# A hybrid attention and RWKV-7 step on one core: projection in other groups of tiles, two products at other places of the recurrence's tile

## What is computed

```python
proj = rms_norm(h, norm_gain) @ w_in            # 2048 prompt rows and 8 x 16 sample rows
att, rcols, g_r = split_projection(proj)        # rcols: 1664 columns
xs = rcols + (prev - rcols) * mix               # prev: the row before, or the stored one
r, k, v, wd, ad = split(xs)
kk = heads(k * k_k)
kk = kk * rsqrt(maximum(sum(kk * kk), 1e-24))   # the sum of squares
y, S = wkv_scan(r, decay, k, v, kk, a, state0)  # the recurrence, per head 64 x 64
y = group_norm(y)
y = y + sum(r * k * r_k) * v                    # the bonus
```

## Time and profile before

| | us |
|---|---|
| median of 3 runs | 1923.75 |
| their range | 1923.07 to 1924.39 |
| the profiled execution | 1919.17 |
| its span, first to last instruction | 1917.4 |
| TensorE busy in the span | 1751.9 (91%) |
| VectorE busy | 859.5 (45%) |
| ScalarE busy | 775.8 (40%) |
| GpSimd busy | 351.7 (18%) |

### The profile page before, as it was taken

The page is one execution under the profiler, slowest core; times in us unless marked ns, Lnnn a source line. Parts: engine busy times, 40 slices in busy tenths (PEclk is TensorE's granted clock), DMA queues, the critical chain, the costliest instruction groups (busy, mean ns, idle before and its releaser), DMA issues. The chain is left out here.

```text
span 1917.4 us, 48732 instructions
## 1 busy us (share of the span) xinstructions
PE 1751.9 (91%) x21474; PEld 1408.2 (73%) x21474; DVE 859.5 (45%) x1195; ACT 775.8 (40%) x1635; POOL 351.7 (18%) x252
## 2 busy tenths in 40 slices
PE   5899999999996999999479999999999998279999
PEld 4677788877885888889357777777777777157787
DVE  5245545455543411211255566556655564143432
ACT  4455555556554321212344444444434431034421
POOL 3010100001000000000123453345334442200000
PEclk9999999999998999999679999999999999679999
DMA  6011111002115412111331212121212110266642
GB/s 220 28 51 34 50 34 50 29 34 67 34 34 203 138 68 93 61 50 43 113 124 48 83 48 60 48 82 48 59 49 82 48 42 22 94 257 237 225 162 105
DMA packets 110977, 160.84 MB, mean 84 GB/s; under 512 B 36272, under 2 KB 70192, under 8 KB 110512
## 3 DMA queue, kind: packets, MB, share of 16 engines
q1 hardware_dynamic: 101408, 143.25, 23.0%
q10 hardware_dynamic: 9360, 14.49, 2.1%
HBM read 103.18 MB, written 55.05 MB: 83 GB/s over the span
## 5 line engine op out<-in xcount | busy, mean ns | idle before, releaser
L935 PE MATMUL j_ps<-j_x_hi,j_w_hi 128*128 128x512 f32 (+1 forms) x520 | 191.3, 368 | 14.6 <-DVE j_x_lo L900 14.6
L935 PE MATMUL j_ps<-j_x_hi,j_w_lo 128*128 128x512 f32 (+1 forms) x520 | 191.0, 367 | 0.0
L935 PE MATMUL j_ps<-j_x_lo,j_w_hi 128*128 128x512 f32 (+1 forms) x520 | 191.0, 367 | 0.0
L565 PE MATMUL a_ps_proj<-a_w_hi,a_x_hi 128*128 128x512 f32 x384 | 158.6, 413 | 2.9 <-ACT a_qk L314 2.8
L565 PE MATMUL a_ps_proj<-a_w_hi,a_x_lo 128*128 128x512 f32 x384 | 158.8, 414 | 0.0
L565 PE MATMUL a_ps_proj<-a_w_lo,a_x_hi 128*128 128x512 f32 x384 | 156.2, 407 | 0.0
L918 DVE SCALAR_TENSOR_TENSOR j_out<-j_ps,j_rest,j_part 128x512 f32<-128x512 f32 (+1 forms) x65 | 43.6, 671 | 238.0 <-ACT j_last_cols L874 208.5
L244 POOL TENSOR_TENSOR a_x_lo<-a_xT,a_x_hi 128x1024 fp32r<-128x1024 f32 x17 | 41.5, 2443 | 486.2 <-ACT a_x_hi L300 486.2
L935 PEld LDWEIGHTS j_ps<-j_x_hi,j_w_hi 128*128 128x128 f32 x520 | 98.5, 189 | 31.0 <-issue 14.8
L2114 PE MATMUL o_ps_y<-o_w_hi,o_z_hi 128*128 128x512 f32 x272 | 111.2, 409 | 7.6 <-DVE o_y L2037 4.0
L1816 PE MATMUL r_ps_gate<-r_gate_w_hi,r_gate_x_hi 128*128 128x512 f32 x272 | 115.3, 424 | 2.3 <-POOL r_gate_x_lo L1339 1.5
(11 more groups left out here) (274 smaller groups left out, 4046.8 us busy)
## 6 DMA issues: line engine op xcount, KB each, us to landing
r_xs<-scratch_xs_T SPq DMA_DIRECT2D x17, 832.0 KB, 6.1
scratch_xs_T<-j_out ACTq DMA_DIRECT2D x52, 256.0 KB, 2.0
scratch_xT<-a_xT SPq DMA_DIRECT2D x17, 512.0 KB, 4.8
r_gate_x_raw<-scratch_xT SPq DMA_DIRECT2D x17, 512.0 KB, 6.7
scratch_gates<-r_gate_out SPq DMA_DIRECT2D x34, 256.0 KB, 2.4
o_g<-scratch_gates SPq DMA_DIRECT2D x17, 512.0 KB, 5.4
a_x<-in_x_prompt SPq DMA_DIRECT2D x16, 512.0 KB, 4.3
j_xT<-scratch_xT SPq DMA_DIRECT2D x4, 2048.0 KB, 8.8
```

Of the source, the lines that this page charges most:

```text
L565: mm = nc.tensor.matmul(ps_proj[:], a[n % 2][:, k, :], w[:, k, g * AW:(g + 1) * AW], start=(k == 0 and i == 0), stop=(k == KT - 1 and i == 2))
L935: mm = nc.tensor.matmul(ps[j][:, 0:n * P], w[:, k, c * P:(c + 1) * P], x[g % 2][:, k, 0:n, :].rearrange("p a n -> p (a n)"), start=(k == 0 ...
```

## The change

In the projection the groups become 4, 4, 3, 3 and 3 tiles. The last one holds prompt tiles 14 and 15 and the sample tile, so groups 2 to 4 have 384 moving columns. There ScalarE does the three prompt operations on the first 256 columns and then the three sample operations on the last 128, and VectorE mixes in two instructions. The two alternating columns in `last_cols` swap places.

In the recurrence the bonus product moves on TensorE from key 33.1 to 11.5 and its copy on ScalarE from 34.4 to 14; in the rotation of the first bank it stands first. The sum of squares moves on TensorE from 34.2 to 31.4 and its reading on VectorE from 35.4 to 33.4.

```diff
@@ -776,12 +776,19 @@
-        GROUPS = TILES // GT
+        SIZES = (4, 4, 3, 3, 3)
+        GROUPS = len(SIZES) - 1
...
         def tiles_of(g):
-            return GT if g < GROUPS else 1
+            return SIZES[g]
+
+        def first(g):
+            return sum(SIZES[:g])
+
+        def prompt_cols(g):
+            return (SIZES[g] - (g == GROUPS)) * P
@@ -858,25 +865,25 @@
-                    if g < GROUPS:
-                        if g > 0:
-                            before = i * 2 + j - SHIFT_TILES
-                            act.wait_ge(parted[before % 2], before // 2 + 1)
-                        nc.scalar.activation(part[j][:, 0:1], last_cols[:, c, g % 2:g % 2 + 1], ACT.Copy, scale=share)
-                        nc.scalar.activation(part[j][:, 1:1 + n * P], ps[j][:, 0:n * P], ACT.Copy, scale=share)
-                        nc.scalar.activation(last_cols[:, c, (g + 1) % 2:(g + 1) % 2 + 1], ps[j][:, n * P - 1:n * P], ACT.Copy).then_inc(parted[j], 1)
-                    else:
-                        now = by_stream(ps[j], SL)
-                        nc.scalar.activation(by_stream(part[j], SL + 1)[:, :, 0], shift_in[:, c, 1:], ACT.Copy, scale=share)
-                        nc.scalar.activation(by_stream(part[j], SL + 1)[:, :, 1:], now, ACT.Copy, scale=share)
-                        nc.scalar.activation(last_cols[:, c, 2:], now[:, :, SL - 1], ACT.Copy).then_inc(parted[j], 1)
+                    n = prompt_cols(g)
+                    if g > 0:
+                        before = i * 2 + j - SHIFT_TILES
+                        act.wait_ge(parted[before % 2], before // 2 + 1)
+                    nc.scalar.activation(part[j][:, 0:1], last_cols[:, c, (g + 1) % 2:(g + 1) % 2 + 1], ACT.Copy, scale=share)
+                    nc.scalar.activation(part[j][:, 1:1 + n], ps[j][:, 0:n], ACT.Copy, scale=share)
+                    last = nc.scalar.activation(last_cols[:, c, g % 2:g % 2 + 1], ps[j][:, n - 1:n], ACT.Copy)
+                    if g == GROUPS:
+                        now, before = by_stream(ps[j][:, n:], SL), by_stream(part[j][:, 1 + n:], SL + 1)
+                        nc.scalar.activation(before[:, :, 0], shift_in[:, c, 1:], ACT.Copy, scale=share)
+                        nc.scalar.activation(before[:, :, 1:], now, ACT.Copy, scale=share)
+                        last = nc.scalar.activation(last_cols[:, c, 2:], now[:, :, SL - 1], ACT.Copy)
+                    last.then_inc(parted[j], 1)
@@ -906,17 +913,18 @@
...
+                    n = prompt_cols(g)
+                    last = nc.vector.scalar_tensor_tensor(out=out[j][:, 0:n], in0=ps[j][:, 0:n], scalar=rest[:, c:c + 1],
+                                                          in1=part[j][:, 0:n], op0=ALU.mult, op1=ALU.add)
                     if g == GROUPS:
...
+                        last = nc.vector.scalar_tensor_tensor(out=by_stream(out[j][:, n:], SL), in0=by_stream(ps[j][:, n:], SL), scalar=rest[:, c:c + 1],
+                                                              in1=by_stream(part[j][:, 1 + n:], SL + 1)[:, :, 0:SL], op0=ALU.mult, op1=ALU.add)
+                    last.then_inc(mixed[j], 1)
@@ -1094,7 +1102,7 @@
-        JOB_ORDER = ((("decay", 0), ("k_tok", -1), ("B0", -1), ("B1", -1), ("bonus", -1), ("v_tok", 0)),
+        JOB_ORDER = ((("bonus", -1), ("decay", 0), ("k_tok", -1), ("B0", -1), ("B1", -1), ("v_tok", 0)),
                      (("iclr", 0), ("b_tok", -1), ("K0", -1), ("K1", -1), ("kk_sum", 0), ("v_swap", 0)))
@@ -1392,12 +1400,13 @@
                 for name, buf in (("v_tok", v_tok), ("v_swap", v_swap), ("k_tok", k_swap), ("b_tok", b_tok)):
+                    if name == "k_tok":
+                        yield 14
+                        ps, read = written(act, t, "bonus")
+                        nc.scalar.activation(bonus[u][:], ps[:, 0:2 * UNITS].rearrange("p (m o) -> p m o", o=2)[:, :, 0], ACT.Copy).then_inc(read, 1)
...
-                yield 34.4
-                ps, read = written(act, t, "bonus")
...
@@ -1463,7 +1472,7 @@
-                yield 35.4
+                yield 33.4
                 ps, read = written(dve, t, "kk_sum")
@@ -1628,7 +1637,7 @@
-                yield 34.2
+                yield 31.4
                 need(pe, t, "kk_sq")
                 ps, done = free_bank(t, "kk_sum")
@@ -1636,6 +1645,14 @@
             def front(t, u, mode):
+                yield 11.5
+                need(pe, t, "rkr")
+                ps, done = free_bank(t, "bonus")
...
@@ -1653,14 +1670,6 @@
-                yield 33.1
-                need(pe, t, "rkr")
-                ps, done = free_bank(t, "bonus")
...
```

More of the change, by code:

```diff
@@ L807, in load_x @@
                 sp.dma_start(xT[:, 0:n].rearrange("p a k n -> p a (k n)"),
-                             io["xT"][g * GT:g * GT + n].rearrange("a p k n -> p a (k n)")).then_inc(x_loaded, 16)
+                             io["xT"][first(g):first(g) + n].rearrange("a p k n -> p a (k n)")).then_inc(x_loaded, 16)
             load_w(0)
@@ L851, in store @@
                 act.wait_ge(mixed[i % 2], i // 2 + 1)
-                act.dma_start(io["xs_T"][c, :, g * (GT * P):(g * GT + n) * P], out[i % 2][:, 0:n * P]).then_inc(stored[i % 2], 16)
+                act.dma_start(io["xs_T"][c, :, first(g) * P:(first(g) + n) * P], out[i % 2][:, 0:n * P]).then_inc(stored[i % 2], 16)
             split_w(0)
@@ L860, in _ @@
             for g in range(GROUPS + 1):
-                n = tiles_of(g)
                 for c, j, i in blocks(g):
@@ L914, in _ @@
                     wait(dve, stored[j], 16 * i)
-                    x, now, before = out[j][:, 0:n * P], ps[j][:, 0:n * P], part[j][:, 0:n * P]
+                    n = prompt_cols(g)
+                    last = nc.vector.scalar_tensor_tensor(out=out[j][:, 0:n], in0=ps[j][:, 0:n], scalar=rest[:, c:c + 1],
+                                                          in1=part[j][:, 0:n], op0=ALU.mult, op1=ALU.add)
                     if g == GROUPS:
-                        x, now, before = by_stream(out[j], SL), by_stream(ps[j], SL), by_stream(part[j], SL + 1)[:, :, 0:SL]
-                    nc.vector.scalar_tensor_tensor(out=x, in0=now, scalar=rest[:, c:c + 1], in1=before, op0=ALU.mult,
-                                                   op1=ALU.add).then_inc(mixed[j], 1)
+                        last = nc.vector.scalar_tensor_tensor(out=by_stream(out[j][:, n:], SL), in0=by_stream(ps[j][:, n:], SL), scalar=rest[:, c:c + 1],
+                                                              in1=by_stream(part[j][:, 1 + n:], SL + 1)[:, :, 0:SL], op0=ALU.mult, op1=ALU.add)
+                    last.then_inc(mixed[j], 1)
                     if g < GROUPS and 0 <= c - 3 < KT:
@@ L1397, in front @@
                     nc.scalar.activation(buf[u][:].rearrange("p m d -> p (m d)"), ps[:], ACT.Copy).then_inc(read, 1)
-                yield 34.4
-                ps, read = written(act, t, "bonus")
-                nc.scalar.activation(bonus[u][:], ps[:, 0:2 * UNITS].rearrange("p (m o) -> p m o", o=2)[:, :, 0], ACT.Copy).then_inc(read, 1)
             def back(t, u, mode):
@@ L1638, in front @@
             def front(t, u, mode):
+                yield 11.5
+                need(pe, t, "rkr")
+                ps, done = free_bank(t, "bonus")
+                for n, c in all_units:
+                    for g in range(2):
+                        last = nc.tensor.matmul(ps[half(g), 2 * unit(n, c):2 * unit(n, c) + 2], c4(rk[:])[half(g), c, chunk(n)],
+                                                const("head_ones")[half(g), g * HD:g * HD + 2], start=True, stop=True)
+                last.then_inc(done, 1)
                 yield 21.8
@@ L1655, in front @@
                     last_k.then_inc(done_k, 1)
-                yield 33.1
-                need(pe, t, "rkr")
-                ps, done = free_bank(t, "bonus")
-                for n, c in all_units:
-                    for g in range(2):
-                        last = nc.tensor.matmul(ps[half(g), 2 * unit(n, c):2 * unit(n, c) + 2], c4(rk[:])[half(g), c, chunk(n)],
-                                                const("head_ones")[half(g), g * HD:g * HD + 2], start=True, stop=True)
-                last.then_inc(done, 1)
             def back(t, u, mode):
```

## The result

| | before | after |
|---|---|---|
| median, us | 1924.07 (4 runs) | 1904.12 (4 runs) |
| range | 1923.07 to 1925.25 | 1902.40 to 1904.27 |
| the profiled execution | 1919.17 | 1902.40 |
| its span | 1917.4 | 1900.6 |

The ratio is 0.9894, with a 95% interval from 0.9877 to 0.9911: 1.1% faster.

What follows compares the result with a forecast made beforehand. The prediction took TensorE's instruction stream to bound both changed places. Projection -12.7, 15 recurrence tiles +5.9, sixteenth tile +1.0 and start +0.3 summed to -5.5 us: 1918.2 us, range 1905.5 to 1928.0.

Steps and rivals of the forecast that it cites:

- Part 1: Projection, groups 2 to 4: 173.1 ns a matmul at 384 columns saves 13.8 us, last block adds 1.1: -12.7 us.
- rival B: Projection: matmul distance on a straight line between 128 and 512 columns, 187.8 ns at 384; total 1932.0 us; chance 7%.
- Part 2's chain: Each recurrence tile: the chain to r_gate_x_lo delays next gate matmuls 0.8 us; tile +0.39 us, 15 tiles +5.9 us.
- Rival A: Recurrence: the chain of r_gate_x_lo does not bind, the turn of v decides; 37.33 us a tile, total 1906.4 us; 15%.
- The +1.0 us for the sixteenth tile: Sixteenth recurrence tile: the bonus product, hidden before in TensorE's wait of 1.53 us, is bare after: +1.0 us.
- The start of the recurrence: Up to the first gate matmuls: up to 1.3 us less, against lower clock and bonus product; put at +0.3 us.
- the risk that the prediction named: Start of the recurrence: TensorE pauses once more, and as long again at half clock speed could cost up to 2 us.
- the last paragraph of the sum: Over 13 recurrence tiles, 11.6 us are TensorE stalls with no releaser that may fall elsewhere when reordered: given +-5 us.
- Rival C: Recurrence: TensorE's stalls without releaser double (+11.6 us), total 1929.8 us; chance 7%.

Runs made afterwards that it cites:

- bonus_only: The kernel before with only the bonus product moved to 11.5 and its copy to 14, as in the kernel after: 1927.46 us, ratio 1.0024.
- small_xs_load: The kernel before, but from the third tile on the load of r_xs brings 64 KB instead of 832 KB: 1910.00 us, ratio 0.9938.

## Why the prediction was wrong, point by point

**Part 1 was right**, in its terms too: 173.0 ns at 384 columns against 173.1, 2.03 us behind the last block against 2.16, -12.9 us in all against -12.7. So rival B's straight line falls, which needed 179 ns to decide. The argument that carried it was the earlier trace rows with the earlier trace rows: find what floors the narrow matmul before drawing a line through it. That there is a floor is shown by 173.0 ns at 384 columns; that the weight load sets it is argued from the earlier trace rows and was not tested. The formula of the Trainium skill cited there ("TensorE: Matmul & The Clock Gate", section "Back-to-back issue gap") gives 162.5 ns at 384 columns; the trace says 173.0, and 110.7 at 128, so regrouping does pay here. The section gives that formula for an isolated matmul, says that it under-counts at small widths, and has 81 ns at 128 and 131 ns at 512 columns for a sustained stream; the prediction left this out. The trace agrees with neither pair (110.7 and 226.0).

**Part 2's chain was right**, and its mechanism as described: `r_gate_x_lo` binds, with 0.85 us of wait where 0.8 was expected, and 6.13 us where 6.11 was worked out. Rival A therefore did not come about. Its number, 1906.4 us, lies near the result by chance only: its tile of 37.33 us is not in the trace. Two terms were a little off. The tile grew by 0.26 us, not 0.39: with the bonus product in it, the stretch between the gate matmuls is 37.95 - 6.13 = 31.82 us, where I had 30.97 + 1.03 = 32.00. And the turn waits for the maximum 0.40 us where 0.7 was expected: it starts 3.07 us behind the sum of squares (3.19 worked out), and TensorE gets there 0.18 us later. That wait bounds nothing, since `r_gate_x_lo` comes later. The +1.0 us for the sixteenth tile measured +0.3 with all that lies behind it, which was not taken apart.

**The start of the recurrence** cost 2.1 us. About 1.0 of it is the bonus product, which now stands ahead of the mark (1086 matmuls up to it instead of 1054). The rest is the clock, the risk that the prediction named with up to 2 us and then priced at almost nothing. The table by stretch before, from the first mark to the gate matmuls and on to the second mark:

```profile
969.24:983.00 13.76, 6.91 (x138) 5.32 (x140) 6.34 (x7) 6.39 (x8) 4.17 (x3) 0.50 0.83 286
983.00:1013.44 30.44, 30.35 (x696) 24.62 (x693) 15.26 (x27) 11.72 (x26) 5.58 (x5) 0.98 0.04 12
```

and after:

```profile
956.46:970.20 13.74, 5.75 (x115) 4.04 (x115) 7.08 (x8) 6.06 (x7) 3.50 (x3) 0.50 0.84 286
970.20:1002.68 32.48, 32.40 (x714) 26.35 (x715) 14.58 (x26) 11.93 (x28) 6.21 (x5) 0.94 0.04 11
```

Both come from the lower level (0.50, 1.2 GHz). Before, TensorE worked on from 979.97 into the gate matmuls, and from 984.1 on these came 0.24 us apart. After, it is done with the turn and the first level at 965.7 and stands idle ahead of the gate matmuls, and they run at the lower level until 974.2:

```profile
970.18 0.79 PE L1825 MATMUL r_ps_gate<-r_gate_w_hi,r_gate_x_hi 128*128 128x512 f32 x1 [4.46 <-POOL r_gate_x_lo L1347]
...
972.18 1.97 PE L1720 MATMUL r_ps_q<-r_w_mat,r_z_mat 64*64 64x64 f32 x32
```

The group of 32 at 972.18 takes 1.97 us where 1.15 is usual; with the four gate matmuls ahead of it at 0.42 us instead of 0.24 that is some 1.5 us at the lower level. The gate matmuls themselves start only 0.5 us earlier, counted from the recurrence's first instruction, of the 1.3 that the prediction had as the most: 1.0 + 1.5 - 0.5 is 2.0.

**The step that failed is the last paragraph of the sum.** It read 11.6 us off, took all of it for stalls without releaser, said that they "may fall elsewhere when the stream is reordered", and gave them +-5 us. In the reading, 2.8 us are lower clock, which the tenths of the earlier trace rows do not show: 3.4 us are a small part of a slice of 48 us. In the bound, a size was known and its cause was not, and nothing supported +-5: a cost whose cause is unknown can go wholly. It went but for 1.7 us (-10.0, most of the 11.3 us between forecast and result in the profiled executions): -7.2 as stalls, since the load of `r_xs` no longer begins where it holds up a packet that TensorE soon needs, and -2.8 as lower clock. In this case's traces the level falls within 0.5 us behind a wait of 0.88 us for the maximum (0.87 in proj_only) six times, in four of the six kernels that have that wait, and never at that place in the eight without it; whether taking the wait away is what ended it was not tested. Rival C had the stalls double and no rival had them go; bonus_only's slowest execution had 21.4 us, so the other side was open too. What would have told was in the same trace: the stall that begins at 1136.4 comes 0.2 us behind the end of a burst that keeps the DMA engines 94% busy, and no instruction packet starts in that burst. The prediction followed the load of `r_xs` as a transfer that slides by 0.86 us and is wanted late. It did not ask what else waits behind it.

Part of the distance between the medians is this too: before, runs spread from 1917.3 to 1928.3 us in the comparisons of this study, small_xs_load from 1909.1 to 1911.1 and the kernel after from 1902.4 to 1904.3. The profiled execution of before was one of its faster ones, so the medians are 20 us apart and the profiles 16.8.

## What to carry over

Where an engine stands still and no semaphore released it, look in the DMA view for its instruction packets, and ask which load lies ahead of them. A reordering that seems to move only work also moves the point of the stream at which a large load begins, and with it these stalls. Bound an unexplained cost by its whole size, to zero and to twice, until its cause is known. And before calling the excess of a tile a stall, look at the granted clock of that tile: two of the seven longer tiles here had no stall at all.

## What was not expected of the hardware

- A 16.4 KB packet of instructions waits for a load that was issued ahead of it: with 1.34 MB in flight it came when the burst ended, 6.1 us behind the first load's issue. With 64 KB + 512 KB it came 3.7 us behind the issue and nothing stalled.
- All 51 waits of TensorE without a releaser, over the 14 tiles of fourteen kernels, stand at one place in a block of 256 instructions and end 2.2 to 2.9 us behind the start of a packet.
- The level of the clock fell for 3.4 us twice in the middle of the recurrence of before, each time behind a wait of 0.88 us, and each time the tile was 1.4 us longer.
- Issuing a load 2.3 us later, with nothing else changed, was worth 0.40% [0.26%, 0.53%] of the kernel.
- At 384 moving columns a float32 part product takes 173.0 ns, 160 for the columns and 13; at 512 it is 226 with the same 13; at 128 it is 110.7.
